# When VectorE mixes the two softmaxes, between expert-row transposes and convolution taps

## The reference

```python
z = rms_norm(x, norm1_g) @ w_in     # columns: GLU-a | GLU-b | q | k | v | two gates
# convolution branch: 31 taps, one weight per channel and tap
u = concat([conv_hist, z_glu_a * sigmoid(z_glu_b)])
c = depthwise_conv(u, w) + b        # then a layer norm, swish, a projection
# attention branch: q1, q2, k1, k2 of width 64, values of width 128
s = where(mask, (q @ k.T) * 64 ** -0.5, NEG_INF)   # one for q1, k1 and one for q2, k2
p = softmax(s)
a = p[:, :, 0] - lam * p[:, :, 1]   # the mix of the two softmaxes
o = rms_norm(a @ v) * (1 - lambda_init)
# later: both branches are gated and added to x, then a retrieval layer: top 16 of
# 16384 single-neuron experts for each of 8 heads, with tables peer_u and peer_v
```

## Time and profile before

| | |
|---|---|
| median of 3 runs | 4311.3 us |
| the profiled execution: its own time | 4312.25 us |
| its span, first to last instruction | 4310.4 us |
| TensorE matmul busy | 4110.0 us, 95% of the span |
| VectorE busy | 3034.5 us, 70% |
| ScalarE busy | 1060.9 us, 25% |
| GpSimd busy | 1442.5 us, 33% |
| granted TensorE clock, mean | 0.972 of full speed |

### The profile page before, as it was taken

One profiled execution on the slowest core, in us unless ns is written; L12 is line 12 of the kernel. 1 busy time (PEld: TensorE's weight loads), 2 busy tenths in 40 slices (PEclk: granted clock), 3 DMA queues, 4 the chain that ended last, 5 costly groups with the idle time before them and its releaser, 6 DMA issues.

```text
span 4310.4 us, 69663 instructions
## 1 busy us (share of the span) xinstructions
PE 4110.0 (95%) x25286; PEld 4014.7 (93%) x25286; DVE 3034.5 (70%) x4447; ACT 1060.9 (25%) x1090; POOL 1442.5 (33%) x682
## 2 busy tenths in 40 slices
PE   8999999999989998999999999999889999999999
PEld 7888888898889998999999999999889999999999
DVE  6876777778756423677637877877468878787874
ACT  3222222222212112222213223232212222222221
POOL 3333232332323332444423333333523323332310
PEclk9999999999999999999979999999999999999999
DMA  7988979979968986866637787778687877777763
GB/s 287 319 310 321 331 273 337 342 261 320 347 223 268 344 309 219 305 224 235 208 137 303 309 317 305 301 309 319 263 315 280 305 287 296 289 294 289 294 255 128
DMA packets 444255, 1225.88 MB, mean 284 GB/s; under 512 B 32800, under 2 KB 256800, under 8 KB 343968
## 3 DMA queue, kind: packets, MB, share of 16 engines
q1 hardware_dynamic: 374224, 881.46, 58.0%
q0 software_dynamic: 36864, 268.45, 15.1%
q10 hardware_dynamic: 32976, 73.47, 4.4%
HBM read 1007.54 MB, written 349.95 MB: 315 GB/s over the span
## 4 chain that ended last, share of the span: by engine, by line
PE 53%; issue 29%; POOL 9%; DVE 6%; DMA 1%; ACT 0%; SPq 0%; POOLq 0%; DVEq 0%; ACTq 0%
PE ST L1710 27%; PE ST L1626 18%; POOL w_lo L551 7%; PE PA L1626 3%; POOL w_lo L543 2%; PE ST L1685 2%; PE PA L1404 2%; PE PA L1636 1%; DVE wk L1234 1%; DMA w_raw<-w_all 1%; DVE cand L1204 1%; DVE wk L1238 0%; DVE isel L1242 0%; DVE ti L1200 0%; DVE wk L1196 0%
## 5 line engine op out<-in xcount | busy, mean ns | idle before, releaser
L624 ACT ACTIVATE w_hi<-w_raw 128x2048 fp32r<-128x2048 f32 x368 | 703.5, 1912 | 1458.5 <-PE ST L1710 786.7
L543 POOL TENSOR_TENSOR w_lo<-w_raw,w_hi 128x2048 fp32r<-128x2048 f32 x133 | 623.8, 4690 | 1154.8 <-ACT w_hi L624 1154.8
L1710 PE MATMUL ST<-wt_hi,w_hi 128*128 128x416 f32 x2048 | 719.4, 351 | 23.3 <-DVE wt_lo L1319 12.7
L1710 PE MATMUL ST<-wt_hi,w_lo 128*128 128x416 f32 x2048 | 724.4, 354 | 0.0
L1710 PE MATMUL ST<-wt_lo,w_hi 128*128 128x416 f32 x2048 | 716.4, 350 | 0.0
L551 POOL TENSOR_TENSOR w_lo<-w_raw,w_hi 128x512 fp32r<-128x512 f32 x280 | 371.4, 1357 | 774.3 <-ACT w_hi L624 774.3
L1404 PE MATMUL PA<-h_hi,w_hi 128*128 128x272 f32 x2496 | 549.4, 302 | 17.8 <-issue 11.8
L581 POOL DMA_INDIRECT rows<-v_rows,v_idx x128 | 312.7, 2443 | 729.5 <-DVE PA L1330 720.8
L1626 PE MATMUL ST<-h_hi,w_hi 128*128 128x416 f32 x1408 | 532.9, 379 | 11.8 <-POOL w_lo L543 11.8
L1404 PE MATMUL PA<-h_hi,w_lo 128*128 128x272 f32 x2496 | 530.0, 295 | 0.0
L1404 PE MATMUL PA<-h_lo,w_hi 128*128 128x272 f32 x2496 | 528.8, 294 | 0.0
(11 more groups left out here) (242 smaller groups left out, 6731.9 us busy)
## 6 DMA issues: line engine op xcount, KB each, us to landing
w_raw<-w_all SPq DMA_DIRECT2D x368, 1024.0 KB
u_in<-w_all SPq DMA_DIRECT2D x128, 1024.0 KB, 8.5
u_rows<-u_out SPq DMA_DIRECT2D x512, 256.0 KB, 7.4
v_rows<-w_all SPq DMA_DIRECT2D x128, 1024.0 KB, 9.1
a_scr<-gb ACTq DMA_DIRECT2D x128, 208.0 KB
g_scr<-g_st ACTq DMA_DIRECT2D x26, 1024.0 KB, 4.4
a_st<-a_scr SPq DMA_DIRECT2D x16, 1664.0 KB
gl_st<-g_scr SPq DMA_DIRECT2D x16, 1664.0 KB, 16.0
```

The source lines that it names most:

```text
L543: pool.tensor_tensor(w_lo[:, slot, :], raw[:, slot, :], w_hi[:, slot, :].bitcast(F32), ALU.subtract)\
L624: act.activation(w_hi[:, slot, :], raw[:, slot, :], ACT.Copy).then_inc(hi_ready, 1)
L1710: last = mm(PD[k], a, r_[b][:, c, :], start=(c == 0 and y == 0), stop=(c == GRP - 1 and y == 2))
```

## The change

In the steps 0 and 1 of each head VectorE's mix now comes ahead of the transpose of expert rows that stood between maximum and mix. In the steps 2 to 4 it comes behind two taps, not behind a transpose and four taps; that first transpose now comes behind four taps and the mix. All instructions are the same, and in the same number.

```diff
@@ -1020,8 +1020,8 @@
                             rope(h, i)
                     for s in range(2):
                         att_max(g + s, s)
+                        att_mix(g + s, s)
                         turn(hp, next(turns))
-                        att_mix(g + s, s)
                         turn(hp, next(turns))
                         evac(hp, r, s + 3)
                     glu(h, (r + 4) % 2)
@@ -1029,10 +1029,11 @@
                     for s in range(2, STEPS):
                         w = 2 + 8 * (s - 2)
                         att_max(g + s, s)
+                        taps(h, w, w + 2)
+                        att_mix(g + s, s)
+                        taps(h, w + 2, w + 4)
                         if r == 0 or s < 4:
                             turn(hp, next(turns))
-                        taps(h, w, w + 4)
-                        att_mix(g + s, s)
                         taps(h, w + 4, w + 6)
                         if r == 0 or s < 4:
                             turn(hp, next(turns))
```

## The result

| | median us | lowest to highest | runs |
|---|---|---|---|
| before | 4317.23 | 4311.20 to 4321.93 | 12 |
| changed | 4327.33 | 4320.16 to 4336.27 | 12 |

The changed kernel takes 1.0025 times as long (95%: 1.0016 to 1.0034), 10.1 us more. The prediction was 4325 against the 4311.3 shown then, a ratio of 1.0032. Over 12 runs the kernel before is 6 us above the three times shown first.

A forecast was written before the change was run, and what follows sets the result against it. The prediction took the chain of VectorE and DMA to bound the first stage. Three pairs at +3.2 us (2.2 + 1.2 + 0.8 - 2.0 + 1.0) and the last at +4.2 gave 13.8 us, 4311.3 to 4325; range 4283 to 4336.

The forecast's parts named there:

- What bounds the stage: First stage: the chain of VectorE and DMA sets each pair's length; TensorE gives back gains at 510.01.
- 30 or less: First stage: TensorE's 61.6 us of waits for the mix fall to 30 us or less, none at step 0.
- Steps 0 and 1: Mix ahead of a transpose, 16 mixes, in VectorE's DMA waits: 0, up to 0.5 us a pair.
- The pushed transpose: Transpose after step 4, first head: new wait of 2.2 us (0 to 3.6) for its buffer, taken as 11.7 us.
- GpSimd, +2.0 us a pair: Steps 2 to 4: GpSimd's pieces meet more taps, +0.4 us a step; +1.2 first head, +0.8 second.
- both terms together: First head: the wait at the transpose after step 4, 2.2 us, and taps held by GpSimd, +1.2 us.
- The last mix: End of a pair's second head: last mix comes 2 taps sooner, -2.0 us, for the first three pairs.
- slower clock: After a pair's last mix: TensorE waits over 2 us, then clocks lower in two pairs of three, +1.0 us.
- the last pair: Fourth pair ends at VectorE, not TensorE, so -2.0 and +1.0 fall away: +4.2 us.
- A: Rival, first stage: TensorE's waits are the bound; 61.6 us and slow clock go, 4225 us; chance 0.08.
- B: Rival, pair ends: only the last mix gets through, 3 x -2.0 = -6 us, 4305 us; chance 0.27.
- C: Rival, taps: GpSimd's pieces move under transposes; -1 us in 20 steps, -2 in 4 tails, 4283; chance 0.10.

The follow-up runs named there:

- the control: The kernel before, unchanged, run and profiled a second time: median 4319.40 us, ratio 0.9997; its profiled execution 4316.89 us.
- the first experiment: Kernel before with only steps 0 and 1 changed (mix ahead of the transpose), steps 2 to 4 as before: 4323.79 us against 4321.46, ratio 1.0008.
- the earlier trace: The kernel before as first profiled, the trace the prediction was read from: profiled execution 4312.25 us, span 4310.4.

## Why the prediction was right, point by point

**What bounds the stage: right.** TensorE's total of waits doesn't decide. It rose, from 95.6 us in the control (mix 60.5, squares 14.0, line 1404 21.1) to 111.5 (58.2, 20.8, and 32.5 for line 1405 with the 9.3 at the end), and removing those at step 0 alone brought no gain. What sets the stage's end is VectorE: its busy time and its waits for stores. Where TensorE waited once at the start of the second head, 3.24 us at 510.01, it now waits three times: 3.05, 1.81 and 2.22 us at 474.01, 492.06 and 515.91.

**"30 or less": wrong.** I had worked out what goes, not what comes. TensorE, which no longer stops at step 0 and whose tiles are done sooner, comes to each next mix earlier by what it gained. The waits that didn't become squares became waits for the next mix. The conclusion, that they are given back, didn't depend on it.

**Steps 0 and 1, 0 up to +0.5 us a pair: not contradicted, not shown.** The first experiment gives +2.3 us in all, with an interval from -1 to +8, and its trace a stage 8.9 us longer. The mix under GpSimd grew by more than I had thought, 3.2 us at 402.45, and was mostly hidden by what I named: the second transpose behind it waits 0.80 us in place of 2.07. That VectorE's new wait for the exponentials (25.4 us in all) falls wholly into the DMA wait is not shown.

**The pushed transpose, +2.2 us: in place, but too large.** The wait is there in all four pairs (5.3 us in all, 8.8 predicted). The room was 9.5 us in each, as I had reckoned; the buffer took 10.1, 9.9, 12.4 and 10.9 us from the end of the transpose, on average 10.8 and not 11.7. With the transpose put back it took 14.6 to 16.0, so this time is no constant of DMA, as I treated it: it holds what stands ahead of the stores in SyncE's order. What the wait costs the kernel is not shown.

**GpSimd, +2.0 us a pair: the place I named was priced right, others were overlooked.** I forecast 8 us more in the taps; 20.2 were measured. Between the transposes a pair of taps now takes 4.89, 5.58 and 4.86 us in the first head's steps 2 to 4 and 4.90 and 5.14 in the second head's two; before, behind them, 4.51, 4.74, 4.52, 4.50 and 4.75. That is +0.47 a step, +0.4 was forecast; times 20 steps 9 us. The rest is step 1's pieces. I counted them only against step 1's mix; but the transpose that opened step 2 lay over their end, and the change moves it away. Its price is 3.08 - 1.97 = 1.1 us in each head (3.08 or 3.09 in all 8), 9 us in 8 heads. Both make 18 of the 20.2. It is the slip that the prediction's own sentence warned of: what is moved out from under a transpose pays. Part is paid back at the head's tail, which I hadn't counted either: the normalisation (lines 999 to 1005) fell from 37.2 to 27.1 us, while the last tap (line 992) rose from 8.0 to 13.7 (control, changed).

**First head, both terms together:** from the transpose at 405.22 to that at 483.19 were 78.0 us. In the changed kernel the four pairs take 78.3, 79.4, 83.4 and 82.2, on average +2.9; +3.4 was predicted. The errors of size cancel in part.

**The last mix, -2.0: right; slower clock, +1.0: right in size by luck.** From the last late transpose to the end of the pair's last mix the four pairs took 50.1 us on average, 51.2 in the control (-1.1; -2.0 + 0.8 predicted). I expected TensorE to wait over 2 us there and to run at its lower clock behind it in two pairs of three. It did so in one: it waits 3.22 us at 610.38, not 0.86, and its granted clock behind is 0.50; in the first and third pair it waits 1.78 and 1.84 us, and the clock behind stays at 1.00, though a wait of 1.58 us had 0.54 behind it in the earlier trace rows. The length of the wait alone doesn't tell. The second and third pair:

```profile
610.40:613.90 3.50, 3.50 (x16) 3.39 (x17) 3.06 (x7) 2.09 (x3) 0.32 (x1) 0.50 0.62 149
910.10:913.60 3.50, 3.49 (x28) 3.43 (x29) 3.06 (x7) 2.09 (x3) 0.64 (x1) 1.00 0.69 133
```

(columns as in the account above). 0.50 is the lower level of 1.2 GHz, 1.00 the upper of 2.4 GHz. From that mix to the evacuation that waits for TensorE (the wait of the earlier trace rows) the time grew against the control by 3.3 us in the second pair and by 0.4 and 0.6 in the others: 1.4 on average, nearly all of it from one pair. In the last pair, as forecast, TensorE's gain doesn't get through: the 9.26 us for the evacuation stand as before.

**Rivals.** A (TensorE's waits are the bound, 4225) is refuted by the first experiment and by the waits. B (only the last mix gets through, 4305) fails at the taps' 20 us, and at its own condition: the buffer was never free after 9.5 us. C (the taps gain under the transposes, 4283) is wrong for this order and right as a lever: with the mix after two taps, both transposes left in place, it gives 24 to 26 us. My argument against it, that the distance from mix to GpSimd is fixed as long as TensorE waits for the mix, holds (3.0 us at 426.61 in the changed kernel, 3.2 at 420.15 with two taps); I hadn't asked what could be put at that distance.

**The total: closer than its terms.** 13.8 us were predicted and 10.1 measured in the medians, but the stage of the two traces compared here grew by 20.2, its four pairs (each from its first transpose to that of the next, the last to the stage's end) by 6.3, -1.9, 6.5 and 8.2 us. The taps' term was too small, the tail was left out, and the terms of the pushed transpose and of steps 0 and 1 are off or unproven. That the median came within 3 us of 4325 is in part luck.

The Trainium skill (GPSIMD Engine Reference, Key points) says that GpSimd shares its SBUF interfaces with VectorE and contends with instructions that run in a 2-port performance mode or have two SBUF inputs. The traces agree for the taps and line 961, which have two such inputs, and for a transpose of one input, which stays at 2.31 us, under pieces or not. Lines 958 and 948 have one tensor as input and are held too (0.37 to 1.47 us, 0.17 to 1.29). The prediction counted the whole mix among the instructions with two inputs; whether those two lines run in a 2-port mode no row here shows.

## What to carry to other kernels

Ask of a wait to be removed not how long it is but where the engine that is freed stops next: 61.6 us of TensorE's waits became 58.2 and the kernel slower. Where another engine holds an instruction of the bounding engine, lay the kinds that aren't held over its spans, and count for each order which instructions stand there. Check the gain against what the covers need themselves: two transposes together cover best and lose it again in waits for their stores. And the time until a buffer is free again isn't the transfer alone: look at what stands ahead of its store in the issuing queue.

## What the runs showed of the hardware that I had not expected

A piece of GpSimd's subtraction (128 x 512, 1.3 to 1.5 us) holds a tiny instruction of VectorE for nearly its own length: line 959 on 128 x 1 took 1.24 us in place of 0.15, line 958 on 128 x 256 1.47 in place of 0.37. The hold goes by instruction more than by element: cutting the pieces frees 38.6 us in the 512-column taps and 40.8 in the 32-column ones, which have a sixteenth of the elements. That the changed order's 20 us fell on the 32-column ones alone (97.7 to 118.1, against 215.4 to 215.2) I can't explain.
